# Seven hand-overs in a hybrid NSA, GLA and MoBA decoder layer: orders, buffers, loads and waits

## What is computed

```python
h = rmsnorm(x, norm_mix_pre[layer])
parts = split(h @ w_in[layer])                 # 17 slices, 7464 columns
o_a = nsa_mixer(...)       # 8 heads: compressed + selected + sliding window
o_b = gla_mixer(...)       # 4 heads, chunked recurrence
o_c = moba_mixer(...)      # 8 heads, block attention
g = sigmoid(merge logits)                      # 3 x 1024 per token
merged = (g[:, :, 0] * (o_a @ w_branch_a[layer])
          + g[:, :, 1] * (o_b @ w_branch_b[layer])
          + g[:, :, 2] * (o_c @ w_branch_c[layer]))
x = x + rmsnorm(merged @ w_out[layer], norm_mix_post[layer])
h = rmsnorm(x, norm_ffn_pre[layer])
gate, up = jnp.split(h @ w_ffn_in[layer], 2, axis=-1)
x = x + rmsnorm((jax.nn.silu(gate) * up) @ w_ffn_out[layer], norm_ffn_post[layer])
```

## Time and profile before

| | us |
|---|---|
| median of three runs | 989.66 |
| lowest, highest | 988.74, 990.40 |
| the profiled execution's own time | 986.35 |
| its span, first to last instruction | 984.6 |
| its mean granted TensorE clock, share of full | 0.992 |

### The profile page before, as it was taken

How to read it: one execution, slowest core, us unless ns; L and a number is a source line. 1 busy time by engine, 2 the same in 40 slices (tenths; PEclk the granted TensorE clock), 3 DMA queues, 4 the chain that set the end, 5 groups by cost and what they waited for, 6 DMA issues and landing times.

```text
span 984.6 us, 13019 instructions
## 1 busy us (share of the span) xinstructions
PE 949.2 (96%) x4708; PEld 793.0 (81%) x4708; DVE 458.3 (47%) x863; ACT 404.0 (41%) x724; POOL 195.9 (20%) x183
## 2 busy tenths in 40 slices
PE   5999999999999999999989998999999999999996
PEld 4888888888788878888878787988888888888884
DVE  6377563331455555556557657222322232333335
ACT  4443353343456656667645343222222222323232
POOL 4443353334133324344310001000000000000000
PEclk9999999999999999999999998999999999999998
DMA  6277135322323222364275451022232323232312
GB/s 228 88 103 173 56 103 197 108 82 90 107 76 102 80 98 70 118 239 131 77 288 188 165 171 65 22 86 93 99 99 93 103 89 107 85 105 88 106 64 87
DMA packets 38029, 111.39 MB, mean 113 GB/s; under 512 B 4116, under 2 KB 8660, under 8 KB 37468
## 3 DMA queue, kind: packets, MB, share of 16 engines
q1 hardware_dynamic: 37692, 110.23, 35.0%
q10 hardware_dynamic: 288, 0.52, 0.2%
HBM read 93.93 MB, written 13.66 MB: 109 GB/s over the span
## 4 chain that ended last, share of the span: by engine, by line
PE 88%; DMA 4%; DVE 3%; ACT 2%; issue 1%; DVEq 0%; POOL 0%; SPq 0%; ACTq 0%
PE bank L1572 26%; PE bank L1574 25%; PE bank L1573 25%; DMA w_raw<-wpack 3%; PE bank L640 3%; PE bank L657 2%; PE bank L632 2%; PE bank L655 1%; PE bank L631 1%; ACT w_hi L893 1%; PE bank L661 1%; DMA gl_in<-gate_logits 1%; PE bank L1608 1%; DMA xs<-x_in 1%; PE bank L1588 1%
## 5 line engine op out<-in xcount | busy, mean ns | idle before, releaser
L1572 PE MATMUL bank<-h_hi,w_lo 128*128 128x512 f32 (+1 forms) x680 | 268.9, 396 | 1.4 <-DVE h_lo L1160 1.4
L1573 PE MATMUL bank<-h_lo,w_hi 128*128 128x512 f32 (+1 forms) x680 | 265.1, 390 | 0.0
L1574 PE MATMUL bank<-h_hi,w_hi 128*128 128x512 f32 (+1 forms) x680 | 265.0, 390 | 0.0
L893 ACT ACTIVATE w_hi<-w_raw 128x1024 fp32r<-128x1024 f32 (+1 forms) x89 | 93.6, 1051 | 162.4 <-PE bank L1574 154.0
L1572 PEld LDWEIGHTS bank<-h_hi,w_lo 128*128 128x128 f32 (+1 forms) x680 | 127.4, 187 | 33.2 <-issue 8.1
L1574 PEld LDWEIGHTS bank<-h_hi,w_hi 128*128 128x128 f32 (+1 forms) x680 | 127.2, 187 | 27.9
L1573 PEld LDWEIGHTS bank<-h_lo,w_hi 128*128 128x128 f32 (+1 forms) x680 | 127.5, 188 | 23.3
L827 POOL TENSOR_TENSOR w_lo<-w_raw,w_hi 128x1024 fp32r<-128x1024 f32 (+1 forms) x37 | 89.0, 2406 | 133.6 <-ACT w_hi L893 133.5
L1081 ACT ACTIVATE w_hi<-w_raw 128x1024 fp32r<-128x1024 f32 x36 | 38.2, 1062 | 152.3 <-PE bank L1574 152.3
L834 POOL TENSOR_TENSOR sc<-sc,ast 128x512 f32<-128x512 f32 (+1 forms) x96 | 66.2, 722 | 140.9 <-DVE ast L545 107.0
L440 ACT ACTIVATE sc<-sc,ast 128x512 f32<-128x512 f32 (+1 forms) x96 | 53.8, 561 | 83.1 <-DVE ast L527 83.1
(11 more groups left out here) (278 smaller groups left out, 1539.0 us busy)
## 6 DMA issues: line engine op xcount, KB each, us to landing
w_raw<-wpack SPq DMA_DIRECT2D x146, 512.0 KB, 3.3
gate_logits<-gl_out SPq DMA_DIRECT2D x24, 256.0 KB, 2.2
gl_in<-gate_logits SPq DMA_DIRECT2D x24, 256.0 KB, 3.7
near_bias<-near SPq DMA_DIRECT2D x1, 3072.0 KB, 33.9
xs<-x_in SPq DMA_DIRECT2D x4, 512.0 KB, 5.9
fullb<-near_bias SPq DMA_DIRECT2D x16, 128.0 KB, 2.5
ckx<-cks SPq DMA_DIRECT2D x16, 128.0 KB, 2.5
ob<-gla_out SPq DMA_DIRECT2D x2, 1024.0 KB, 6.1
```

The lines of the kernel that those rows point to most:

```text
L893: sa.activation(split_weights(c)[0][:, 0:n], raw[:, s, 0:n], ACT.Copy).then_inc(w_hi, 1)
L1572: mm(out, ll, rh, start=start, stop=False, skip_group_check=True)
L1573: mm(out, lh, rl, start=False, stop=False, skip_group_check=True)
L1574: return mm(out, lh, rh, start=False, stop=stop, skip_group_check=True)
```

## The change

Seven edits, none of which adds or removes arithmetic:

1. **Order in the norms.** DVE does `transposed_lo(0)` and `(1)` both behind `residual(2)`; `(1)` stood behind `residual(3)`. `transposed_lo(2)` goes ahead of `lo(C_FIN + 4)`.
2. **Own buffers for the last two weight chunks** and for the activations that go with them.
3. **Order of loads.** `xr` is loaded in four DMAs behind products 8 and later, and the two norm rows behind those; they stood ahead of the fetches and logits.
4. **Finer waits.** `w_out` chunk m = 0 waits for 22 products and m = 1 for 24.
5. **The near bias in eight parts** of two rows, behind `fetch(10)` to `fetch(17)`.
6. **Key low halves behind the first units.** The low halves of the last `ck` chunk go behind DVE's unit 0, those of gate chunk 38 behind unit 1, and `far_bias` goes to the place of chunk 27.
7. **Compressed keys one chunk later** (and the transposes of their bias with them).

```diff
+NEAR_PARTS = 8
...
-        for name, first, kib in (("out", C_OUT + 4, 72), ("gate0", C_FIN, 168), ("gate1", C_FIN + 2, 184)):
+        for name, first, kib in (("out", C_OUT + 4, 72), ("gate0", C_FIN, 168), ("gate1", C_FIN + 2, 184),
+                                 ("last", N_CHUNKS - 2, 168)):
...
+        ash_last = at(184, "as_hi_last", [P, 2, SEQ], F32R)
+        asl_last = at(188, "as_lo_last", [P, 2, SEQ], F32R)
...
+            elif c in (N_CHUNKS - 2, N_CHUNKS - 1):
+                eng.wait_ge(w_used, C_FIN + 4)
...
+                    if u == 0:
+                        stacked_low(C_MERGE - 1)
+                    if u == 1:
+                        lo(C_GATE + 1)
...
-                if c == 10:
-                    sp.wait_ge(near_ready, 18)
-                    sp.dma_start(near_dram, near[64:80, :].unsqueeze(1).broadcast_to([16, P, D_NEAR])).then_inc(near_out, 16)
+                if 10 <= c < 10 + NEAR_PARTS:
+                    if c == 10:
+                        sp.wait_ge(near_ready, 18)
+                    n = 16 // NEAR_PARTS
+                    h = n * (c - 10)
+                    sp.dma_start(near_dram[h:h + n], near[64 + h:64 + h + n, :].unsqueeze(1).broadcast_to([n, P, D_NEAR])
+                                 ).then_inc(near_out, 16)
...
-            sp.dma_start(xr[:, :, :], x_d.rearrange("(t p) d -> p t d", p=P)).then_inc(xr_in, 16)
-            sp.dma_start(wpost[:, :], rows_d[0, :, :]).then_inc(posts_in, 16)
-            sp.dma_start(wfpre[:, :], rows_d[1, :, :]).then_inc(posts_in, 16)
...
+                if 4 <= j < 4 + NT:
+                    t = j - 4
+                    sp.dma_start(xr[:, t, :], x_d[t * P:(t + 1) * P, :]).then_inc(xr_in, 16)
+                elif 4 + NT <= j < 6 + NT:
+                    row = j - 4 - NT
+                    sp.dma_start((wpost, wfpre)[row][:, :], rows_d[row, :, :]).then_inc(posts_in, 16)
...
-                if c + 2 >= C_MERGE:
+                if c == FIRST_MOBA + 2:
+                    ve.wait_ge(cmp_ready, 9)
+                    far_bias(ve, 0)
+                    far_bias(ve, 1)
+                if c + 2 == C_MERGE:
                     lo(c + 2)
...
-                else:
-                    transposed_lo(ve, t - 2)
+                elif t == 2:
+                    transposed_lo(ve, 0)
+                    transposed_lo(ve, 1)
...
+            transposed_lo(ve, 2)
             lo(C_FIN + 4)
-            transposed_lo(ve, 2)
             transposed_lo(ve, 3)
...
-                if c == C_O + 5:
+                if c == C_O + 6:
...
-                    if m == 0 and t == 2:
-                        te.wait_ge(d_free, N_GATES)
+                    if m < 2 and t == 2:
+                        te.wait_ge(d_free, N_GATES - 2 + 2 * m)
```

More of the change, by code:

```diff
@@ L1084, in act_hi @@
                 sa.wait_ge(f_free, k + 3)
-                if k >= 2:
+                if k >= NF - 2:
+                    sa.wait_ge(w_used, C_FIN + 4)
+                elif k >= 2:
                     sa.wait_ge(w_used, C_FOUT + k - 1)
-                sa.activation(ash[:, k % 2, :], act[:, k, :], ACT.Copy).then_inc(a_hi, 1)
+                sa.activation(split_act(k)[0], act[:, k, :], ACT.Copy).then_inc(a_hi, 1)
             for f in range(NF - 2, NF):
@@ L1248, in gla_pick_own, with stacked_low @@
                                    ).then_inc(aux_free[AUX_AT["lv7"] % 2], 1)
+            def stacked_low(c):
+                kind, j = STRAIGHT[c]
+                order = [x for x in STRAIGHT if x[0] in ("ks", "kw", "aq", "cq", "ck")]
+                first, second, factor = stacked(kind, j)
+                for half, (hi_, lo_, of) in enumerate((first, second)):
+                    ve.wait_ge(s_hi, 8 + 2 * order.index((kind, j)) + half + 1)
+                    ins = ve.scalar_tensor_tensor(out=lo_, in0=of(single_bank(c)), scalar=factor,
+                                                  in1=hi_.bitcast(F32), op0=ALU.mult, op1=ALU.subtract)
+                ins.then_inc(s_free[SINGLE[c] % 2], 1)
             for c in range(C_MERGE):
@@ L1278, in _ @@
                                      ALU.add).then_inc(done, 1)
-                elif kind in ("ks", "kw", "aq", "cq", "ck"):
-                    order = [x for x in STRAIGHT if x[0] in ("ks", "kw", "aq", "cq", "ck")]
-                    first, second, factor = stacked(kind, j)
-                    for half, (hi_, lo_, of) in enumerate((first, second)):
-                        ve.wait_ge(s_hi, 8 + 2 * order.index((kind, j)) + half + 1)
-                        ins = ve.scalar_tensor_tensor(out=lo_, in0=of(ps), scalar=factor, in1=hi_.bitcast(F32),
-                                                      op0=ALU.mult, op1=ALU.subtract)
-                    ins.then_inc(done, 1)
+                elif kind in ("ks", "kw", "aq", "cq", "ck") and c < C_MERGE - 1:
+                    stacked_low(c)
                 elif kind == "nv" and j == 1:
@@ L1506, in act_lo @@
                 ve.wait_ge(a_hi, k + 1)
-                ve.tensor_tensor(asl[:, k % 2, :], act[:, k, :], ash[:, k % 2, :].bitcast(F32),
-                                 ALU.subtract).then_inc(a_lo, 1)
+                high, low = split_act(k)
+                ve.tensor_tensor(low, act[:, k, :], high.bitcast(F32), ALU.subtract).then_inc(a_lo, 1)
             for f in range(NF - 2, NF):
@@ L1847, in down_half @@
             def down_half(k, t, half, start, stop):
-                b, bw = k % 2, (C_FOUT + k) % 2
-                cols = slice(512 * half, 512 * half + 512)
-                return three(bank[4 * half + t][:, :], ash[:, b, t * P:t * P + P], asl[:, b, t * P:t * P + P],
-                             wh[:, bw, cols], wl[:, bw, cols], start, stop)
+                (ah, al), (high, low) = split_act(k), split_weights(C_FOUT + k)
+                cols, mine = slice(512 * half, 512 * half + 512), slice(t * P, t * P + P)
+                return three(bank[4 * half + t][:, :], ah[:, mine], al[:, mine], high[:, cols], low[:, cols],
+                             start, stop)
             def down(k, t, start, stop):
```

24 lines of the change are left out of this document (12 added, 12 removed).

## The result

The changed kernel takes 1017.3 us (median of four runs, 1014.61 to 1018.57) against 989.2 for the kernel before (986.19 to 990.40): ratio 1.0275, 95% interval 1.0242 to 1.0307. It is **slower**, by some 28 us. The forecast was 1027.6, 10.3 too much, and inside its range; direction and mechanism held. The profiled execution took 1014.61 us, 28.26 more than that of before.

What follows compares the result with a forecast made beforehand. PE, busy for 96% of the span, plus its waits was taken to bound the kernel. 986.35 + 60.5 (slow parts and clock) - 22.6 (six hand-overs) = 1024.3, plus 3.3 to the median: 1027.6 us, range 1005 to 1052.

Steps and rivals of the forecast that it cites:

- Engines of a part: Near bias: a part of two source rows runs on 2 DMA engines instead of 16, the same two each time.
- First in, first out, and the place: Loads land behind near-bias parts issued ahead; PE waits at nearly each chunk from 90 to 200 us, DMA share near 0.13.
- Start and cadence: Chunks 11 to 18: 3.1 us before transfer, then 17.0 us per part and fetch (15.7 + 1.3); chunk 18 lands at 192.8.
- The reason for 15.7: Time of one near-bias part in us: middle by ratio between 8.0 (weight-load engine rate) and 30.8 (old near-bias rate).
- the swap: A transfer of 64 partitions at 187 GB/s over 16 engines, 11.7 each, by which a part would take 16.8 us.
- From `hi(18)` to the matmul: Chunk 18: its first matmul comes 8.2 us after its load lands, between 6.2 and 8.7, so at 201.0, +58.2 us.
- Low clock behind: PE's clock is low after the last of the chunk waits, costing 2.3 us, for +60.5 in all.
- The six: Six hand-overs remove PE waits of 16.3 us and 6.3 us of low clock behind them, a gain of 22.6 us.
- the 0.6 us in the norms: Norms: tile 1's `h_lo` would end at 602.9, 0.6 us ahead of PE, the only slack counted as thin.
- Parts cost nothing: Rival: near-bias parts have 16 engines or take 8.0 us on two, only gains are left, 965.7 us; chance 0.17.
- An engine keeps 6.4 GB/s: Rival: a near-bias part takes 30.8 us, cadence 32.1, chunk 18 starts at 321.8, total 1148 us; chance 0.03.
- Gaps stay: Rival: parts cost as forecast, but another gap of the same size stands behind each closed one, 1050 us; chance 0.02.

Runs made afterwards that it cites:

- e3: The changed kernel with eight near-bias parts of 384 KB at the same places, each taking all 16 rows: 961.84 us, ratio 0.9666.
- e4: The changed kernel with four near-bias parts of four rows, behind fetch(10) to fetch(13): 1021.1 us, ratio 1.0262.
- e5: The changed kernel with eight parts of two rows each, rows eight partitions apart instead of neighbouring: 961.88 us, ratio 0.9729.
- e1: The changed kernel with the near bias in one part again, the six other hand-overs kept: 963.78 us, ratio 0.9704.
- e6 to e11: e3 with one hand-over undone each: norms 968.87 us, last chunks 966.56, loads 967.50, finer waits 964.36, keys 965.31, attention 965.59.
- e12: The changed kernel with its eight two-row parts spread behind fetch(10), 13, 16, 19, 23, 27, 31 and 35: 961.52 us, ratio 0.9688.

## Right and wrong, step by step

- **Engines of a part.** Right: two (short packets in e3), and the same two (when each part began).
- **First in, first out, and the place.** Right: the waits are from 106 to 193 us, `w_hi` waits for `w_raw`, the DMA share between loads is 0.13, and the parts from the second on took 24 to 29 us from issue to their last packet.
- **Start and cadence.** The transfers started where the sum put them, 55.8 (the DMA share falls to 0.12 by 56). The cadence was put at 17.0 and is (185.55 - 56.8) / 8 = 16.1, with the 1.0 of `cbt` taken off. This is the term that was mis-sized: 8 x 0.9 = 7.2 us too much. The part itself was near (15.7 against 15.8 by the packets); wrong was to add the weights' 1.3 in full, since the next part's packets begin 0.0 to 0.9 us behind the last one's. Packets of the two interleave.
- **The reason for 15.7.** It was a middle between an engine's two rates, set beside the swap. e4 and e5 show that an engine's rate is not the limit: with two far rows an engine is as fast as in weight loads (the bound of 8.0, measured 7.9). The value came out right by luck, the reason did not; what is named beside it, one port for four neighbours with 15.4, fits all the runs but is not told apart from the rows' place in DRAM.
- **From `hi(18)` to the matmul.** 8.2 taken, 7.05 measured (192.60 - 185.55). `gr` ended 6.2 behind `hi(18)` as in the earlier trace rows; behind it came only the four transposes of the last tile, 0.9 us to the matmul, where the sum left 2.0 for all sixteen. 1.1 us too much.
- **Low clock behind.** 2.3 against 1.6, 0.7 too much. In the bad stretch itself the low clock made PE's work 13.1 us longer. The sum did not need that term: the loads set the pace there, so it only filled time in which PE would have waited.
- **The six.** 22.6 against 23.3 between profiled executions, 0.7 too little. Each took its own wait, nothing stood close behind, and the 0.6 us in the norms that was called thin was enough. That this fits so well is in part luck: the rows come from an execution of before with a high clock, and against the medians of e1's group the six bring 32.7.
- **Together:** 7.2 + 1.1 + 0.7 + 0.7 = 9.7, the difference of the profiled executions (1024.3 forecast, 1014.6 measured); the other 0.6 is median against profiled, 2.7 instead of 3.3.
- **The rivals.** "Parts cost nothing" put 965.7 for parts of 8.0 us on two engines; e5 has just these parts and takes 961.9. "An engine keeps 6.4 GB/s" is out for two rows (12.4 GB/s), though with four rows it is nearly so (6.8). "Gaps stay" is out by e1 and by e6 to e11. The break-even at a part of 11.0 us lies between e5 (8) and the changed kernel (15.8); no run is nearer.

## What to carry to other kernels

Splitting a DMA can make it slower: count the slowest dimension of each part, which set its engines here, and the neighbouring rows in it, which set its rate. A queue of loads behind such parts is held by the most loaded engine, so weigh its work per load against the time between two loads; cut along a dimension that keeps all rows in each part (e3), take rows far apart (e5), or space the parts (e12), and 961.5 to 961.9 us come out of the same edits that gave 1017.3. And a short wait of TensorE is to be priced with the low clock behind it: 4.7 us cost 7 to 8.

## What the runs showed of the hardware

SP, which only issues, was held as well. In the changed kernel's timeline of SP (start, us, DMA issued):

```profile
74.99 2.15 SPq L734 DMA_DIRECT2D near_bias<-near  x1
77.19 16.07 SPq L740 DMA_DIRECT2D cbt<-distance_bias  x2
142.16 14.54 SPq L707 DMA_DIRECT2D w_raw<-wpack  x1
```

The pair of `cbt` took 16.07 us to issue, and a single fetch up to 14.54. In e3 the pair took 3.93, a fetch 0.33 to 0.36, and a part 0.43 instead of 2.1. It does not take two overloaded engines: in the kernel before, with the one near bias on all sixteen, the pair took 8.80. So the issue of a DMA waits while the engines have a backlog, and here it waited longest when two of them did. It was not on the path, as those two engines' packets ran on with gaps of 0.9 us at most, but another DMA of that queue would have been late. The second surprise is how much neighbouring rows slow each other down: the packet of 1536 bytes takes 65, 110 or 190 ns with one, two or four rows of a group of four in use at once.
